# Keeping the residual in SBUF in front of a Fourier mixer, running the channel DFT group by group behind the fold, and placing two kinds of small work later in an RG-LRU output map

## The chip, the cores and the metric

The kernel runs on the 8 cores of one Trainium2 chip. Each core computes one of the 8 batch elements; the cores exchange nothing. The metric is the device time of the slowest core in microseconds (us). Every figure of the trace is from the slowest core of one profiled execution, core 4.

## The reference

A backbone of two layers works on 2048 latent tokens of 2048 channels per batch element (256 context tokens run beside them up to the first mixer). Each layer is: half-step SwiGLU, token mixer, half-step SwiGLU. The mixer of layer 0 is a bidirectional RG-LRU, that of layer 1 a grouped Fourier transform. Every sub-layer takes an RMSNorm of its input, shifts and scales it by adaLN terms, and adds the gated RMSNorm of its output to the residual stream x:

```python
def ffn_sublayer(x, g_pre, g_post, shift, scale, gate, w_in, w_out):
    y = swiglu(modulate(rmsnorm(x, g_pre), shift, scale), w_in, w_out)
    return x + MACARON * gate * rmsnorm(y, g_post)

def fourier_mixer(h, w_out):
    hg = h.reshape(bsz, n, N_FGROUPS, FGROUP).astype(jnp.float32)
    f = jnp.fft.fftn(hg, axes=(1, 3), norm='ortho').real
    return f.reshape(bsz, n, D_MODEL).astype(h.dtype) @ w_out
...
        hx = modulate(rmsnorm(x, g[2]), sh2, sc2)
...
        x = x + gt2 * rmsnorm(y, g[3])
```

So a sub-layer's residual update needs the norm of its whole output y, and the next pre-norm the norm of the whole updated x.

## The kernel before

Activations lie channel-major: 16 chunks of 128 channels (KC = 16, index m or kc) by tokens. The residual lives in DRAM (`xs`), sub-layer outputs too (`ys`). Tokens are worked in tiles of 1024 (two halves of 512). The program is written out by hand: the order in which Python emits instructions is the order on each engine, and waits are semaphores derived from tile accesses. DMAs issued by SP (SyncE) carry activations, those issued by POOL (GpSimd) weights and constants; each issuer's DMAs start in its program order, and an issuer that waits holds up all that stands behind it.

A normal feed-forward phase streams weights and lets the matmuls run; the residual update of the other tile is woven in step by step (`post_steps`: a piece of y and x of 128x512 is loaded to the ring `xl`, updated, stored, squared and summed).

Two places matter here.

**The RG-LRU output map** (`rglru`, function `mix_y`, called for tiles i = 0 and 1). For each of 16 output chunks m PE does 32 matmuls (`mix_mm`, L1013), ScalarE copies the result out of PSUM (L1119), SP stores it to `ys` (L1121), ScalarE squares it (L1126), and PE adds the squares up by a matmul with ones (L1132); that last matmul is kept in the list `pend` and comes one chunk later. While tile 0 is mapped, the residual of tile 0 is loaded to SBUF (`Resident.load_x`, L647, 16 tiles `xm`, two DMAs each); while tile 1 is mapped, `Resident.post` updates that residual, two chunks per m for m = 1 to 8: two VectorE operations (L668, L672), a square on ScalarE (L676), and the matmul with ones on PE (L682), which `post` issues at once. Then come the scale of the next norm, the modulated input of the feed-forward, and the stores of the residual.

**The front of the Fourier mixer.** The transform folds position t with 2048 - t. Tile 0 (positions 0 to 511 and 1536 to 2047) is folded inside the last feed-forward phase (`fold_steps(F, 0)`). After that phase `fourier` runs on an idle PE: `carry` (32 steps of `post_steps` for tile 1, positions 512 to 1535, with sums on PE, L414), the scale of the norm, `stage1` for the four position blocks of tile 0, the loads and folds of tile 1 (`fold_steps(F, 1)`, 16 steps), `stage1` for the blocks 4 to 8. `stage1(nb)` is the channel DFT: for one block of 128 positions all 8 channel groups, cosine part (L1348 with 128 columns, L1351 with one) to `U`, sine part (L1366) to `V`. Block 8 is the single position 1024. `stage2` is the position DFT of `U` with the constant `Cn` and of `V` with `Sn`; its first matmul of the sine part needs `V` and `Sn`. `Cn`, `Sn` and the first output weights `wf` are loaded by POOL ahead of `carry`.

Of the kernel before, what the change touches and what calls it, by code (L numbers as in the profile page):

```python
# [180 lines left out]
def build(nsub=6):  # L181
# [96 lines left out]
    hgb = S.sbuf("hgb", [128, 64], F32)  # L278
    qtb = S.sbuf("qtb", [128, 1], F32)
# [360 lines left out]
    class Resident:  # L640
# [21 lines left out]
        def post(self, m, slot):  # L662
# [21 lines left out]
            S.op("pe", stat, reads=[ry, r_const], writes=spair_res(slot))  # L684
# [35 lines left out]
    def rglru(W0, tl, hx, hcb, r_hxs, tiles):  # L720
# [384 lines left out]
        def mix_y(i, ky, sched):  # L1105
            pend = []
            for m in range(KC):
# [6 lines left out]
                while pend:  # L1114
                    pend.pop(0)()
# [41 lines left out]
        def begin():  # L1157
            for _ in range(yr.n - 1):
# [17 lines left out]
        sched = {m + 1: [lambda m=m, i=i: R.post(2 * m + i, kp[0]) for i in range(2)] for m in range(8)}  # L1176
# [3 lines left out]
        mix_y(1, ky, sched)  # L1180
# [64 lines left out]
    def fold_steps(F, t):  # L1245
        ta, tb, nb_ = ((0, 1536, 512), (512, 1024, 513))[t]
        q = []

        def load(kc):
            out = []  # L1250
            for (t0, w) in ((ta, 512), (tb, nb_)):
                b, rb, dn = xl.next()
                S.dma("sp", dn, lambda e, b=b, t0=t0, w=w: e.dma_start(out=b[:, :w], in_=xs[kc, :, t0:t0 + w]),
                      reads=X_s.r(kc, t0, w), writes=[rb])
                out += [b, rb, rb.gen]
            q.append(out)

        def mk(kc):
            def f():
# [3 lines left out]
                if kc + 2 < KC:  # L1263
# [3 lines left out]
                S.op("dve", lambda e: e.tensor_tensor(out=xa[:, :512], in0=xa[:, :512], in1=rsx[t][:, 0:512],  # L1267
                                                      op=ALU.mult), reads=[r_rsx[t]], writes=[ra])
                S.op("dve", lambda e: e.tensor_tensor(out=xb[:, :512], in0=xb[:, :512], in1=rsx[t][:, 512:1024],
                                                      op=ALU.mult), reads=[r_rsx[t]], writes=[rb])  # L1270
                if t == 0:
                    S.op("dve", lambda e: e.tensor_copy(out=xb[:, 512:513], in_=xa[:, 0:1]), reads=[ra], writes=[rb])
                else:
                    S.op("dve", lambda e: e.tensor_tensor(out=xb[:, 512:513], in0=xb[:, 512:513],
                                                          in1=rsx[0][:, 512:513], op=ALU.mult),
                         reads=[r_rsx[0]], writes=[rb])
                    S.op("act", lambda e: e.activation(out=F.hx[:, kc, 0:1], in_=xb[:, 0:1], func=AF.Identity,
                                                       bias=modcol(1, 3, kc, 0), scale=dercol(1, 1, 0, 0, kc)),
                         reads=[rb, r_der] + r_modq(1, 3), writes=[F.r_hx])
# [6 lines left out]
                S.op("act", lambda e: e.activation(out=F.H[t][0][:, kc, :], in_=pb[:], func=AF.Identity,  # L1286
                                                   bias=sh2[:, kc:kc + 1], scale=dercol(1, 1, 0, 0, kc)),
                     reads=[rp, r_der, r_sh2], writes=[F.r_H[t][0][kc]])
                S.op("act", lambda e: e.activation(out=F.H[t][1][:, kc, :], in_=xa[:, :512], func=AF.Copy,
                                                   scale=dercol(1, 1, 0, 0, kc)),  # L1290
                     reads=[ra, r_der], writes=[F.r_H[t][1][kc]])
# [355 lines left out]
```

How the kernel before makes its waits and increments, by code:

```python
    def _wait(self, stream, ev):  # L89
        if ev is None:
            return
        key, val = ev
        if self.seen[stream].get(key, 0) >= val or (stream == "pe" and key == "E_pe"):
            return
        self.seen[stream][key] = val
        self.eng[stream].wait_ge(self.sems[key], val)
# [16 lines left out]
    def op(self, stream, fn, reads=(), writes=()):  # L113
        self._deps(stream, reads, writes)
        ins = fn(self.eng[stream])
        key = "E_" + stream
        self.cnt[key] += 1
        ins.then_inc(self.sems[key], 1)
        ev = (key, self.cnt[key])
        self._commit(ev, reads, writes)
        return ev
# [1 line left out]
    def dma(self, stream, dsem, fn, reads=(), writes=()):  # L123
        self._deps(stream, reads, writes)
        key = "D_" + dsem
        sem = self._sem(key)
        inss = fn(self.eng[stream])
        if not isinstance(inss, (list, tuple)):
            inss = [inss]
        for ins in inss:
            ins.then_inc(sem, 16)
            self.cnt[key] += 16
        ev = (key, self.cnt[key])
        self._commit(ev, reads, writes)
        return ev
```

## Time and profile before

| | us |
|---|---|
| runs shown | 9951.44 (median), 9933.07, 11277.62 |
| profiled execution | 9958.34 |
| its span, slowest core (core 4) | 9957.0 |
| spans of the other cores | 9864.1 to 9951.5 |

The time of an execution is the span of the slowest core and 1.3 us around it. The run of 11277.62 is of a disturbed kind and is not compared with. PE (TensorE) is busy 89% of the span, so what can move is where it stands idle. The rows further down are read so: a timeline row has start, duration, engine, line of the kernel, operation and tiles, and in square brackets how long the engine stood idle before it and what ended that; rows named POOLq or SPq, or DMA_DIRECT2D on POOL, are issues of DMAs, not transfers. The granted clock PEclk is a share of 2.4 GHz; 0.5 is the lower level of 1.2 GHz.

### The profile page before, as it was taken

How to read it: one execution, taken by the hardware profiler on the slowest of the kernel's cores; microseconds unless marked ns; L12 is line 12 of the kernel's file. 1: busy time of each engine (PE TensorE's matmuls, PEld its weight loads, DVE VectorE, ACT ScalarE, POOL GpSimd, SP SyncE). 2: the span in 40 equal slices, each digit the busy share in tenths (PEclk: the TensorE clock that was granted, in tenths of full speed). 3: DMA queues.
4: the chain of work that ended last, by engine and by line, in shares of the span. 5: the costliest groups of instructions: out<-in, count | busy, mean ns of one | idle time of the engine just before them, and what ended most of it. 6: DMA issues, size and time to landing. Idle time of an engine off the chain costs nothing.

```text
span 9957.0 us, 124360 instructions; the slowest of 8 cores (9864.1 to 9957.0 us)
## 1 busy us (share of the span) xinstructions
PE 8893.2 (89%) x47440; PEld 4372.1 (44%) x48079; DVE 2410.6 (24%) x3408; ACT 2016.8 (20%) x2999; POOL 614.1 (6%) x983
## 2 busy tenths in 40 slices
PE   2999999997886889999999999999965499999994
PEld 1665555653332334444444444444423144444442
DVE  1111211213886212111211221122124322111102
ACT  1111111123775311111111111111113211110000
POOL 0000000000111000000000000000000000000000
PEclk9999999998998999999999999999977799999997
DMA  8778878887445677567766996677565676566545
GB/s 165 140 127 169 162 132 159 162 153 168 90 85 134 148 159 144 113 133 149 150 122 139 176 185 130 136 148 146 118 164 150 169 144 139 109 135 121 119 90 140
DMA packets 517609, 1399.41 MB, mean 141 GB/s; under 512 B 63640, under 2 KB 193816, under 8 KB 464032
## 3 DMA queue, kind: packets, MB, share of 16 engines
q0 software_dynamic: 152352, 830.83, 49.6%
q1 hardware_dynamic: 364672, 560.58, 19.1%
q8 instruction: 391, 6.41, 0.3%
q14 instruction: 194, 1.59, 0.1%
HBM read 1979.48 MB, written 221.25 MB: 221 GB/s over the span
## 4 chain that ended last, share of the span: by engine, by line
PE 79%; DMA 10%; ACT 3%; DVE 3%; issue 2%; SPq 1%; DVEq 0%; ACTq 0%; POOL 0%; POOLq 0%
PE PS L178 48%; PE PS L598 25%; PE PS L1013 2%; PE PS L798 1%; DMA w_36_90<-modw 1%; PE PS L883 1%; DVE gM_49_21458 L917 1%; DMA wfs<-ev_26_80 1%; PE PS L349 1%; SPq L647 1%; DMA wfs<-ev_27_81 0%; DMA ys<-ev_26_80 0%; DMA xl_21_75<-ys 0%; PE PS L393 0%; DVE gB_47_21456 L914 0%
## 5 line engine op out<-in xcount | busy, mean ns | idle before, releaser
L408 DVE TENSOR_TENSOR acc_16_70<-acc_16_70,sq_29_83 128x512 f32<-128x512 f32 (+1 forms) x135 | 87.4, 648 | 2007.7 <-ACT sq_29_83 L407 1957.1
L178 PE MATMUL PS<-hb_28306,w_90_28303 128*128 128x512 bf16 x2381 | 536.2, 384 | 4.8 <-ACT acc_16_70 L397 1.8
L178 PE MATMUL PS<-hb_28306,w_89_28302 128*128 128x512 bf16 x2315 | 521.6, 384 | 3.8 <-issue 0.5
L178 PE MATMUL PS<-hb_28306,w_88_28301 128*128 128x512 bf16 x2128 | 475.7, 382 | 15.1 <-DVE mods_3_45 L356 11.8
L178 PE MATMUL PS<-hb_28306,w_87_28300 128*128 128x512 bf16 x2127 | 476.9, 383 | 3.4 <-issue 0.5
L178 PE MATMUL PS<-hb_28306,w_91_28304 128*128 128x512 bf16 x2069 | 462.6, 382 | 2.5
L178 PE MATMUL PS<-hb_92,w_34_88 128*128 128x384 bf16 x2048 | 344.1, 330 | 45.4 <-ACT hb_92 L474 32.3
L178 PE MATMUL PS<-hb_92,w_36_90 128*128 128x384 bf16 x2176 | 361.3, 327 | 12.5 <-DVE mods_2_44 L356 12.3
L178 PEld LDWEIGHTS PS<-hb_28306,w_90_28303 128*128 128x128 bf16 x2432 | 239.4, 99 | 294.1 <-issue 33.0
L178 PE MATMUL PS<-hb_92,w_35_89 128*128 128x384 bf16 x2176 | 361.2, 327 | 1.5 <-ACT ev_28_82 L571 1.2
L178 PEld LDWEIGHTS PS<-hb_28306,w_89_28302 128*128 128x128 bf16 x2368 | 232.7, 99 | 283.7 <-issue 26.9
L178 PE MATMUL PS<-hb_92,w_33_87 128*128 128x384 bf16 x2048 | 341.0, 328 | 2.5 <-ACT ev_26_80 L571 2.5
L178 PEld LDWEIGHTS PS<-hb_28306,w_88_28301 128*128 128x128 bf16 x2176 | 213.0, 98 | 269.6 <-issue 25.2
L178 PEld LDWEIGHTS PS<-hb_28306,w_87_28300 128*128 128x128 bf16 x2176 | 213.4, 99 | 258.5 <-issue 16.8
L571 ACT ACTIVATE ev_28_82<-PS 128x512 f32<-128x512 f32 (+1 forms) x266 | 148.6, 559 | 840.2 <-PE PS L178 789.7
L571 ACT ACTIVATE ev_26_80<-PS 128x512 f32<-128x512 f32 (+1 forms) x262 | 145.9, 557 | 845.8 <-PE PS L178 797.4
L178 PEld LDWEIGHTS PS<-hb_28306,w_91_28304 128*128 128x128 bf16 x2112 | 206.9, 98 | 251.0 <-issue 15.4
L571 ACT ACTIVATE ev_27_81<-PS 128x512 f32<-128x512 f32 (+1 forms) x264 | 147.4, 558 | 827.4 <-PE PS L178 789.6
L178 PEld LDWEIGHTS PS<-hb_92,w_34_88 128*128 128x128 bf16 x2048 | 201.6, 99 | 181.3 <-issue 51.5
L178 PEld LDWEIGHTS PS<-hb_92,w_36_90 128*128 128x128 bf16 x2176 | 213.1, 98 | 154.2 <-issue 14.3
L178 PEld LDWEIGHTS PS<-hb_92,w_35_89 128*128 128x128 bf16 x2176 | 212.9, 98 | 144.0 <-issue 5.2
L598 PE MATMUL PS<-hid_28305,w_90_28303 128*128 128x512 bf16 x1164 | 263.9, 384 | 5.2 <-DVE hid_28305 L573 1.9
(763 smaller groups left out, 12355.1 us busy)
## 6 DMA issues: line engine op xcount, KB each, us to landing
w_90_28303<-win POOLq DMA_DIRECT2D x38, 1024.0 KB, 10.1
w_89_28302<-win POOLq DMA_DIRECT2D x37, 1024.0 KB, 9.9
w_35_89<-win POOLq DMA_DIRECT2D x34, 1024.0 KB, 10.9
w_36_90<-win POOLq DMA_DIRECT2D x34, 1024.0 KB, 10.7
w_87_28300<-win POOLq DMA_DIRECT2D x34, 1024.0 KB, 11.1
w_88_28301<-win POOLq DMA_DIRECT2D x34, 1024.0 KB, 11.0
w_91_28304<-win POOLq DMA_DIRECT2D x33, 1024.0 KB, 10.3
w_34_88<-win POOLq DMA_DIRECT2D x32, 1024.0 KB, 10.7
```

The source lines that it names most:

```text
L178: ins = e.matmul(out, l, r, start=(i == 0), stop=(i == n - 1))
L349: ins = e.matmul(o, w, scb[:, 2 * c:2 * c + 2], start=(c == 0), stop=(c == KC - 1))
L408: S.op("dve", lambda e: e.tensor_tensor(out=a, in0=a, in1=sb[:, :n], op=ALU.add), reads=[rsq], writes=[r_acc])
L571: S.op("act", lambda e, tb=tb, h=h, k=ks[0]: e.activation(out=tb[:, :n], in_=sbank(k, h, n), func=AF.Silu), reads=[rPS[2 * ks[0] + h]], wr ...
L598: ins = e.matmul(sbank(k, h, n), buf[:, (c - a) * 128:(c - a + 1) * 128], rhs(c, h), start=(c == 0), stop=(c == nk - 1))
L647: S.dma("sp", f"xr{m}", lambda e: [e.dma_start(out=self.xr[m][:, off:off + w], in_=src.ap[m, :, t0:t0 + w]) for (off, w, src, dst, t0, whi ...
L798: ins = e.matmul(sbank(k, b % 2, 512), buf[:, kk * 256 + o:kk * 256 + o + 128], hx[:, kk, b * 512:(b + 1) * 512], start=(kk == 0), stop=(k ...
L883: ins = e.matmul(PS[:, 3072 + h * 512:3584 + h * 512], wg(d, g), vcb[:, lo + h * 512:lo + (h + 1) * 512], start=True, stop=True)
L917: S.op("dve", lambda e: e.tensor_tensor_scan(out=f(gM[d]), data0=f(gA[d]), data1=f(gB[d]), initial=0.0, op0=ALU.mult, op1=ALU.add), reads= ...
L1013: ins = e.matmul(sbank(k, h, 512), buf[:, c * 128:(c + 1) * 128], zt[i][:, c, h * 512:(h + 1) * 512], start=(c == 0), stop=(c == KC - 1))
```

## The change

1. In `mix_y` of tile 0, `load_x(m)` no longer stands for all 16 chunks ahead of the loop: chunk m's load is issued in the loop behind the stores of chunk m.
2. `Resident.post` can hand its matmul with ones to the caller's list `pend`. In `mix_y` of tile 1 it does, so that these come behind the next chunk's 32 matmuls, beside the sum that was there already. `begin` loads 3 pieces of y ahead instead of 4, since a buffer is now held longer.
3. In `fourier`, the residual update of tile 1 is done by `Resident` on whole chunks of 1024 columns: 3 pieces of y and all 16 of x are queued on SP, x stays in SBUF (`xf`, in the room of `U`, `V`, `Cn` and `Sn`), and the stores of it follow. The fold of tile 1 reads `xf`; one of its two halves, the subtraction, goes to POOL. `c16` is the one column (position 1536) that the fold needs from tile 0, fetched for all chunks by one DMA.
4. `stage1` goes by channel group instead of position block. Groups 0 to 5 stand inside the fold, in pairs, behind its chunks 10, 12 and 14; groups 6 and 7 behind it. `Cn` and `Sn` are loaded behind the fold and behind the stores of the residual whose room they take.

```diff
-        for m in range(KC):
-            R.load_x(m)
-        mix_y(0, 3, {})
+        mix_y(0, 3, {m: [lambda m=m: R.load_x(m)] for m in range(KC)}, [])
...
-            S.op("pe", stat, reads=[ry, r_const], writes=spair_res(slot))
+            go = lambda: S.op("pe", stat, reads=[ry, r_const], writes=spair_res(slot))
+            if pend is None:
+                go()
+            else:
+                pend.append(go)
...
+        for m in range(KC):
+            if m < yr.n - 1:
+                R.load_y()
+            R.load_x(m)
...
+        ks = hold_slot()
+        rstd(accs[0], r_accs[0], 512, slot=ks)
+        for m in range(KC):
+            R.post(m, ks)
+        rstd(rsx[1], r_rsx[1], 512, ks)
+        held.discard(ks)
+        for m in range(KC):
+            R.store(m)
...
+        def fold1(m):
+            tb, rt, _ = yr.next()
+            S.op("dve", lambda e: e.tensor_tensor(out=tb[:, :1024], in0=xr[m][:], in1=rsx[1][:], op=ALU.mult),
+                 reads=[r_rsx[1], r_xr[m]], writes=[rt])
+            S.op("dve", lambda e: e.tensor_copy(out=tb[:, 1024:1025], in_=c16[:, m, :]), reads=[r_c16], writes=[rt])
...
+            S.op("dve", lambda e: e.tensor_tensor(out=pb[:], in0=tb[:, :512], in1=xv, op=ALU.add), reads=[rt], writes=[rp])
+            S.op("pool", lambda e: e.tensor_tensor(out=qb[:], in0=tb[:, :512], in1=xv, op=ALU.subtract), reads=[rt], writes=[rq])
...
+        for m in range(KC):
+            fold1(m)
+            if m == 9:
+                handover(r_xr[:9], r_Us + r_U8 + r_V)
+            if m >= 10 and m % 2 == 0:
+                for g in {10: (0, 1), 12: (2, 3), 14: (4, 5)}[m]:
+                    stage1(g)
+        handover(r_xr[8:13], [r_Cn])
+        handover(r_xr[13:] + yr.res[3:], [r_Sn])
         S.dma("pool", "fcn", lambda e: e.dma_start(out=Cn[:], in_=cn3), writes=[r_Cn])
...
+        stage1(6)
+        stage1(7)
-        for st in carry:
-            st()
```

Where the change moves instructions is seen best in the queues of the engines. In SP's queue at the start of the output map of tile 0, the kernel before has sixteen pairs of `xm` loads and then the stores of the loop; this is the end of the loads:

```order
L647 DMA xm_107_28320<-xs 128x512 x2
L647 DMA xm_108_28321<-xs 128x512 x2
L647 DMA xm_109_28322<-xs 128x512 x2
L1121 DMA ys<-ev_26_80 128x512
L1121 DMA ys<-ev_27_81 128x512
```

With the change the stores of a chunk stand ahead of one load (names count one lower, `xm_93` is the first residual chunk):

```order
L1045 DMA zt_80_22235<-zs 128x7x512 x4
L1124 DMA ys<-ev_25_79 128x512
L1124 DMA ys<-ev_26_80 128x512
L646 DMA xm_93_28306<-xs 128x512 x2
L1124 DMA ys<-ev_27_81 128x512
L1124 DMA ys<-ev_25_79 128x512
L646 DMA xm_94_28307<-xs 128x512 x2
```

On PE at the start of the output map of tile 1 (`zt` is the mixer's result, `wm` a weight; `sq` with `onesb` the sum over y, `ym` with `onesb` that over the residual), before:

```order
L1013 MATMUL PS<-zt_81_22236,wm_82_22237 128x512 x32
L1013 MATMUL PS<-zt_81_22236,wm_83_22238 128x512 x32
L1132 MATMUL PS<-sq_29_83,onesb_48 128x512 x2
L682 MATMUL PS<-ym_110_28323,onesb_48 128x512 x2
L682 MATMUL PS<-ym_111_28324,onesb_48 128x512 x2
L1013 MATMUL PS<-zt_81_22236,wm_84_22239 128x512 x32
```

and with the change, where the first two sums over the residual stand one chunk's 32 matmuls later:

```order
L1016 MATMUL PS<-zt_80_22235,wm_81_22236 128x512 x32
L1016 MATMUL PS<-zt_80_22235,wm_82_22237 128x512 x32
L1135 MATMUL PS<-sq_28_82,onesb_48 128x512 x2
L1016 MATMUL PS<-zt_80_22235,wm_83_22238 128x512 x32
L1135 MATMUL PS<-sq_29_83,onesb_48 128x512 x2
L681 MATMUL PS<-ym_109_28322,onesb_48 128x512 x2
L681 MATMUL PS<-ym_110_28323,onesb_48 128x512 x2
```

On POOL in front of the Fourier mixer, before, the constants follow the small fills at once:

```order
L1323 MEMSET hxx_59040 128x2048
L1324 MEMSET Ux_59051 128x1152
L1325 MEMSET Wx_59052 128x2048
L1326 DMA Wx_59052<-fwx 8x2048
L1327 DMA Cn_59043<-cn 128x9216
L1328 DMA cnx_59054<-cn 128x9
```

With the change sixteen subtractions of the fold (L1363, the last two shown) stand ahead of them:

```order
L1363 TENSOR_TENSOR sq_28_82<-yf_151_59076 128x512
L1363 TENSOR_TENSOR sq_29_83<-yf_152_59077 128x512
L1415 DMA Cn_59046<-cn 128x9216
L1416 DMA cnx_59057<-cn 128x9
L1417 DMA Sn_59053<-sn 128x8192
```

## Rows read from the trace of the kernel before

**Rows 1.** The page: its first line, and the chain that ended last by engine.

```profile
span 9957.0 us, 124360 instructions; the slowest of 8 cores (9864.1 to 9957.0 us)
...
PE 79%; DMA 10%; ACT 3%; DVE 3%; issue 2%; SPq 1%; DVEq 0%; ACTq 0%; POOL 0%; POOLq 0%
```

**Rows 2.** Windows: length, engines' busy time, granted clock, DMA share, GB/s.

```profile
2380.00:2440.00 60.00, 21.84 (x72) 6.28 (x70) 38.24 (x53) 20.23 (x26) 0.00 (x0) 0.60 0.92 292
3190.00:3226.00 36.00, 0.69 (x3) 0.28 (x3) 0.00 (x0) 2.33 (x4) 0.53 (x1) 0.55 0.95 275
3226.00:3330.00 104.00, 98.80 (x438) 44.17 (x446) 0.00 (x0) 30.92 (x44) 6.88 (x13) 0.96 0.65 137
3345.00:3452.00 107.00, 79.49 (x302) 31.75 (x306) 29.58 (x24) 31.22 (x40) 4.23 (x8) 0.89 0.52 143
3452.00:3546.00 94.00, 51.83 (x237) 22.37 (x241) 18.78 (x17) 35.56 (x41) 5.16 (x9) 0.77 0.92 196
7356.00:7488.00 132.00, 19.50 (x35) 3.90 (x35) 47.51 (x66) 25.55 (x39) 9.53 (x11) 0.53 0.82 244
7488.00:7500.00 12.00, 11.75 (x193) 11.47 (x193) 6.20 (x11) 8.80 (x10) 0.00 (x0) 0.73 0.62 176
7548.00:7562.00 14.00, 12.25 (x225) 12.28 (x227) 5.13 (x5) 5.68 (x6) 0.00 (x0) 0.84 0.00 1
```

**Rows 3.** Timeline, output map of tile 0: SP, ScalarE and PE around its third chunk.

```profile
3188.99 1.03 PE L1013 MATMUL PS<-zt_80_22235,wm_84_22239 128*128 128x512 bf16 x4
...
3215.17 0.42 SPq L1121 DMA_DIRECT2D ys<-ev_26_80  x1
...
3223.66 0.60 ACT L1119 ACTIVATE ev_26_80<-PS 128x512 f32<-128x512 f32 x1 [34.76 <-DMA ys<-ev_26_80]
...
3226.55 9.21 PE L1013 MATMUL PS<-zt_80_22235,wm_85_22240 128*128 128x512 bf16 x31 [0.22 <-issue]
```

**Rows 4.** Timeline of PE in the output maps of tile 0 and then tile 1.

```profile
3257.61 0.59 PE L1132 MATMUL PS<-sq_30_84,onesb_48 128*128 128x512 bf16 x2
...
3264.95 0.59 PE L1132 MATMUL PS<-sq_29_83,onesb_48 128*128 128x512 bf16 x2
...
3386.67 0.59 PE L1132 MATMUL PS<-sq_30_84,onesb_48 128*128 128x512 bf16 x2
...
3390.13 0.59 PE L682 MATMUL PS<-ym_111_28324,onesb_48 128*128 128x512 bf16 x2 [2.86 <-ACT ym_111_28324 L676]
...
3400.10 0.59 PE L1132 MATMUL PS<-sq_29_83,onesb_48 128*128 128x512 bf16 x2
```

**Rows 5.** Timeline of VectorE: residual updates of 1024 columns in the same map.

```profile
3337.12 1.22 DVE L668 TENSOR_TENSOR ym_112_28325<-ym_112_28325,acc_86_28299 128x1024 f32<-128x1024 f32 x1
...
3339.71 1.22 DVE L668 TENSOR_TENSOR ym_113_28326<-ym_113_28326,acc_86_28299 128x1024 f32<-128x1024 f32 x1
```

**Rows 6.** DMA issues from 3150 to 3560: KB each, median us from issue to landing.

```profile
ym_112_28325<-ys SPq DMA_DIRECT2D x3, 512.0 KB, 6.9
```

**Rows 7.** Timeline of PE, both ends of the Fourier mixer's front.

```profile
7346.36 9.66 PE L598 MATMUL PS<-hid_28305,w_91_28304 128*128 128x512 bf16 x44
...
7563.65 1.89 PE L178 MATMUL PS<-Sn_59050,V_59042 128*128 128x512 bf16 x8
```

**Rows 8.** Timeline of POOL and VectorE in the RG-LRU loop.

```profile
2611.87 4.50 POOL L922 TENSOR_TENSOR gM_50_21459<-gM_50_21459,gM_49_21458 128x2048 f32<-128x2048 f32 x1 [11.06 <-DVE gM_50_21459 L917]
...
2613.15 5.65 DVE L897 SCALAR_TENSOR_TENSOR gB_47_21456<-gB_47_21456,vcB_21463 128x2304 f32<-128x2304 f32 x1 [1.43 <-ACT gB_47_21456 L887]
...
2624.82 2.55 DVE L897 SCALAR_TENSOR_TENSOR gB_48_21457<-gB_48_21457,vcB_21463 128x2304 f32<-128x2304 f32 x1
```

**Rows 9.** DMA issues from 7340 to 7600, columns as in rows 6.

```profile
Cn_59043<-cn POOLq DMA_DIRECT2D x1, 2304.0 KB, 12.3
...
Sn_59050<-sn POOLq DMA_DIRECT2D x1, 2048.0 KB, 17.6
...
cnx_59054<-cn POOLq DMA_DIRECT2D x1, 2.2 KB, 12.0
```

More of the change, by code:

```diff
@@ L1113, in mix_y @@
                     mix_mm(m, i, k, range(KC))
-                while pend:
-                    pend.pop(0)()
+                for f in list(pend):
+                    f()
+                pend.clear()
                 load_wm(i * KC + m + 4)
@@ L1157, in begin @@
         def begin():
-            for _ in range(yr.n - 1):
+            for _ in range(yr.n - 2):
                 R.load_y()
@@ L1266, in f @@
                 assert ra.gen == ga and rb.gen == gb
[L1267 to L1279, printed above, removed]
+                S.op("dve", lambda e: e.tensor_tensor(out=xa[:, :512], in0=xa[:, :512], in1=rsx[0][:, 0:512],
+                                                      op=ALU.mult), reads=[r_rsx[0]], writes=[ra])
+                S.op("dve", lambda e: e.tensor_tensor(out=xb[:, :512], in0=xb[:, :512], in1=rsx[0][:, 512:1024],
+                                                      op=ALU.mult), reads=[r_rsx[0]], writes=[rb])
+                S.op("dve", lambda e: e.tensor_copy(out=xb[:, 512:513], in_=xa[:, 0:1]), reads=[ra], writes=[rb])
                 pb, rp, _ = ev.next()
@@ L1301, in fourier @@
         o += 4096
+        X0 = o
         U = sb_at("U", [128, 9, 1024], BF16, o)
@@ new lines, in stage1, with pe_u, pe_v @@
+        def stage1(g):
+            hs = [F.H[0][0], F.H[1][0]]
+            ms = [F.H[0][1], F.H[1][1]]
+            rp = [F.r_H[t][0][2 * g + jj] for t in range(2) for jj in range(2)]
+            rm = [F.r_H[t][1][2 * g + jj] for t in range(2) for jj in range(2)]
+            lhs = lambda H, nb, jj: H[nb // 4][:, 2 * g + jj, (nb % 4) * 128:(nb % 4) * 128 + 128]
+            ku = next_slot()
+            kv = next_slot()
+            def pe_u(e):
+                ins = None
+                for nb in range(9):
+                    w = lambda jj: lhs(hs, nb, jj) if nb < 8 else F.hx[:, 2 * g + jj, :]
+                    o = ku * 1024 + nb * 128 if nb < 8 else k8 * 1024
+                    for jj in range(2):
+                        e.matmul(PS[:, o:o + 128], w(jj), ccs[:, jj, 0:128], start=(jj == 0), stop=(jj == 1))
+                    o = kx * 1024 + nb * 8 + g
+                    for jj in range(2):
+                        ins = e.matmul(PS[:, o:o + 1], w(jj), ccs[:, jj, 128:129], start=(jj == 0), stop=(jj == 1))
+                return ins
+            S.op("pe", pe_u, reads=rp + [r_cc, F.r_hx], writes=spair_res(ku) + [rPS[2 * kx], rPS[2 * k8]])
+            gs = slice(g * 128, (g + 1) * 128)
+            S.op("act", lambda e: e.activation(out=U[:, 0:8, gs], in_=PS[:, ku * 1024:(ku + 1) * 1024].rearrange(
+                "p (b f) -> p b f", f=128), func=AF.Copy), reads=spair_res(ku), writes=[r_Us[g]])
+            S.op("act", lambda e: e.activation(out=U[:, 8, gs], in_=PS[:, k8 * 1024:k8 * 1024 + 128], func=AF.Copy),
+                 reads=[rPS[2 * k8]], writes=[r_U8[g]])
+            def pe_v(e):
+                ins = None
+                for nb in range(8):
+                    o = kv * 1024 + nb * 128
+                    for jj in range(2):
+                        ins = e.matmul(PS[:, o:o + 128], lhs(ms, nb, jj), ccs[:, jj, 129:257], start=(jj == 0), stop=(jj == 1))
+                return ins
+            S.op("pe", pe_v, reads=rm + [r_cc], writes=spair_res(kv))
+            S.op("dve", lambda e: e.tensor_copy(out=V[:, :, gs], in_=PS[:, kv * 1024:(kv + 1) * 1024].rearrange(
+                "p (b f) -> p b f", f=128)), reads=spair_res(kv), writes=[r_V[g]])
@@ L1376, in fourier @@
-        for nb in range(4):
-            stage1(nb)
-        for st in fold_steps(F, 1):
-            st()
-        for nb in range(4, 9):
-            stage1(nb)
+        stage1(6)
+        stage1(7)
+        handover(yr.res[:3], xl.res)
         S.op("dve", lambda e: e.tensor_copy(out=Ux[:, :, 0:8], in_=PS[:, kx * 1024:kx * 1024 + 72].rearrange(
```

125 lines of the change are left out of this document (55 added, 70 removed).

## The prediction, made before the change was run

> **What bounds the kernel now.** I read the page's chain of waits first: 79% of the 9957.0 us span runs through PE, 10% through DMA [rows 1]. So PE's matmuls set the time, the change leaves their number as it is, and it can only win where PE stands idle beside its three edits. The windows give the size of these places [rows 2]. From 3190 to 3226 PE is busy 0.69 of 36 us while the DMA engines are busy 0.95. From 3345 to 3452 it is busy 79.5 of 107 us. From 7356 to 7488 it is busy 19.5 of 132, and up to 7562 two blocks of 12 us and 14 us follow with 48 us between them. Then the timeline, for what ends each wait. In the output map of tile 0 PE stops at 3190.0 and goes on at 3226.55, because ScalarE waits 34.76 us for one store of y, which SP issues at 3215.17, behind 32 loads of the residual [rows 3]. In the map of tile 1 the period from one sum over y to the next is 3400.10 - 3386.67 = 13.43 us, where in that of tile 0 it is 3264.95 - 3257.61 = 7.34 us [rows 4]: behind the 32 matmuls PE waits 2.86 us for the square of the residual, and the rest of a period runs at less than the full clock, for the granted clock of this stretch is 0.89 [rows 2]. In front of the Fourier mixer the last feed-forward matmul ends at 7346.36 + 9.66 = 7356.02, and the first matmul that needs `V` and `Sn` starts at 7563.65 [rows 7]: 207.6 us, in which PE has 24.0 us of channel DFT (11.75 + 12.25 [rows 2]) and some sums.
>
> **Edit 1, the loads of the residual behind the stores.** The two stores of a chunk no longer queue behind 32 loads, so the fourth chunk can start when the third ends: 3226.55 - 3190.02 = 36.5 us at most. The price is that 8.4 MB now have to pass while PE works. In the idle stretch the DMA engines were busy 0.95 x 36 = 34 us; were all of that residual, the stretch from 3226 to 3330 would go from 0.65 x 104 = 68 to 102 us of 104 [rows 2]. It just fits, and the stores and weights are wanted a chunk or more later. SP now has one load of 0.5 MB ahead of each chunk's stores, a wait of about 2 us at 275 GB/s, with 7.3 us to hide in. Ends: 20 (the map becomes DMA-paced for part of its length) and 36.5. I take **34**, near the end that the store order gives, less something for the crowd.
>
> **Edit 2, sums one chunk later.** A chunk with the sums of two residual chunks is the 7.34 us period plus four matmuls of 512 columns; 32 + 2 of them make 7.34, so four cost 0.86, and the chunk is 8.2 us if nothing else binds. Eight chunks carry them: 8 x (13.43 - 8.2) = 41.8 us. What could bind next: VectorE needs 2 x 2.59 us a chunk [rows 5], below 8.2. DMA is busy 0.52 x 13.43 = 7.0 us a chunk, which is 0.85 of 8.2. The y pieces are fetched three ahead instead of four, and each load waits until the buffer's sum has run: from there 6.9 us of landing [rows 6], 2.6 of VectorE and about 3 of ScalarE make 12.5, against two chunks, 16.4. If the landing doubled, the chunk would be about 10 and the gain 27. Ends 20 and 42; I take **40**. The tail of this map (3452 to 3546, DMA busy 0.92 [rows 2]) stores the residual and loads the next weights. Its order stays, and it keeps its length.
>
> **Edit 3, the front of the Fourier mixer**, as a chain from 7356.0:
> - The scale and the first loads are as before. On SP 3 pieces of y and 16 of x now stand ahead of the fourth y: 19 x 0.524 = 10 MB. At 275 GB/s, as the residual loads of rows 2 went, that is 36 us; at 244 or 292 (the lowest and highest of the load stretches there) 41 or 34. Begun at about 7359, the fourth y lands at 7397.
> - Updates 3 to 15 go at VectorE's pitch of 2.59 [rows 5], 34 us, to 7431. The ring of 4 just covers a landing of 6.9 us. Square, sums and two steps of the scale: 5 us, 7436. The stores (8.4 MB, 31 us) run beside the fold and must be done for the first nine chunks before `U` is written; they are, near 7467.
> - The fold: VectorE has 1.22 for 1024 columns, about 0.7 for 512, and some 0.3 for the single column and gaps, 2.25 us. The subtraction on POOL is 4.50/4 = 1.13 us, by the row of 2048 columns [rows 8]. Whether the two run side by side decides. The rows say no: a VectorE operation with two SBUF operands that starts 1.3 us into POOL's takes 5.65 us, where the same form alone takes 2.55, that is, it ends as if begun when POOL's was over (2616.4) [rows 8]. So a chunk is 3.4 us if they never overlap, and 2.7 if only VectorE is held, since the subtraction and the addition become ready together and only the difference of 1.13 and 0.7 is added. I take 3.4, for 16 chunks 54 us; with 2.7 it is 43.
> - Three pairs of `stage1` inside the fold. They are not beside the fold: ScalarE's copies and VectorE's casts wait for PE, and the next chunk of the fold queues behind them. All 416 DFT matmuls took 24.0 us at clocks of 0.73 and 0.84 [rows 2]. A pair is a quarter: 6 us at that clock, 8.6 at the lower level, plus a cast of 1.2 and hand-overs. I take 9, 27 for three: 7436 + 54 + 27 = 7517.
> - Then `Cn`, its last column and `Sn` are issued, behind the sixteenth subtraction on POOL. `Sn` landed 17.6 us after its issue beside other traffic [rows 9]; 4.5 MB at 292 GB/s are 15. I take 17 and 1 for the issues: 7535. The last pair hides behind that.
>
> Gain 7563.65 - 7535 = **28 us**. Ends: none at all (244 GB/s, and pairs at 14 us, as they come with PE at the lower level and every copy in series), and 48 (292 GB/s, chunks of 2.25, pairs of 8).
>
> A rule bears on the fold. The Trainium skill, page "SBUF — State Buffer", section "Who interferes with whom", states that a VectorE instruction with two SBUF inputs and a GpSimd one that reads SBUF exclude each other for the whole instruction, and that the order of issue decides which is blocked. By it the chunk is 3.4 us, which the rows above show for one of the two orders; with the side-by-side reading (2.7) the sum below would be 11 us shorter.
>
> Costed at nothing: `c16`, 2048 elements fetched by SP at the start of the last feed-forward phase. A DMA of 1152 such elements landed after 12.0 us, and the large `Cn` ahead of it took as long [rows 9], so about 21 us at most; the fold of tile 0 behind it has a whole phase of 16 chunks to catch up. Without that cover VectorE would be late by these 21 us. The 8.4 MB that the old fold read again are gone with no gain of their own, since their time is in the chain.
>
> **Sum.** 9958.3 (the profiled execution) - 34 - 40 - 28 = 9856. The median of the runs shown lies 7 us lower, so 9849; I say **9850**. By the ends: 36.5 + 42 + 48 = 126 gives 9825, 20 + 20 + 0 gives 9911.
>
> **The rivals**, on the basis of the median.
> - *The front gains nothing.* Pairs and fold in series, then the constants, eat what the saved reads give: 9951 - 74 = 9877. For it: all three consumers wait in one queue order, and PE starts each pair after idling, at 0.55 of the clock (rows 2 show that value for idle stretches). Against: 8.4 MB less, and updates on 1024 columns at 2.59 us, where the 32 old steps took 132 us. Chance 0.17.
> - *POOL and VectorE overlap, or the constants come fast.* The front gains 45: 9951 - 119 = 9832. For: the two operands of the subtraction were read by nobody else in rows 8. Against: the held operation there. Chance 0.14.
> - *The sums still wait.* y lands too late with 3 ahead and a busier queue, edit 2 gives 10: 9879. Here the change does not do what it says. Against: 16.4 us for 12.5. Chance 0.07.
> - *DMA becomes the bound, and the kernel is slower.* If transfers in these places cannot exceed the 137 to 143 GB/s that the two maps show [rows 2], the 8.4 MB cost 61 us in the map of tile 0 against 36 saved; its neighbour, with the same 15 MB, gains nothing; and the front, whose 17 MB of loads are then read in 122 us and whose stores hold up `U` for another 61, ends near 7600 instead of 7563.65. 25 + 38 = 63 us more: 10014. It decides from the point where a chunk of the first map needs over 7.3 us of DMA. Against: 275 and 292 GB/s in the same rows. Chance 0.04.
>
> My forecast has the remaining 0.58. The range 9805 to 9900 takes in the forecast's ends but for the worst, the first three rivals, and the 18 us between the two undisturbed runs; the fourth rival and a part of the tails stay out. All ends together save 126 us, and 2% of 9951 is 199 us (about what a measurement of this kernel can tell from no change), so within 2% it is in nearly every case: faster by over 2% 0.02, within 0.96, slower 0.02.
>
> **What would show it.** Edit 1: ScalarE's copy in the map of tile 0 no longer waits some 35 us for a store, and the DMA share of the map nears 0.9. Edit 2: the residual's sums on PE have no wait on ScalarE, and the period is near 8.2. Edit 3: VectorE's update operations 2.6 us apart from the fourth on; in the fold, additions or subtractions longer than alone and a pitch of 3.4; three gaps of about 9 us on VectorE ended by PE; the first matmul on `Sn` released by its DMA. I would be wrong if the stores of y are late again behind single loads, if the subtraction runs beside the addition, or if `stage1` takes far more than 9 us a pair.

## The result, and the profile after

The changed kernel took 9818.26 and 9825.11 us, the kernel before 9933.07 and 9951.44 us: ratio 0.9879, 95% interval 0.9836 to 0.9921, some 120 us or 1.2% less. (The four runs of the change have a median of 10136.3 us, because in two of them one or both dies ran at a lowered clock, for which the forecast has no term; such dies are left out of every total below, and the profile shown is that of a later run of the same kernel without them.) The forecast was 9850 within 9805 to 9900, "within 2%" with 0.96. For these two times the direction and the range held; the gain was 120 us instead of 102, and its parts were not those of the forecast.

The page of the changed kernel, first line and chain:

```profile
span 9817.0 us, 124059 instructions; the slowest of 8 cores (9771.0 to 9817.0 us)
...
PE 77%; DMA 11%; DVE 4%; ACT 3%; issue 3%; SPq 1%; DVEq 0%; POOL 0%; ACTq 0%; POOLq 0%
```

PE's share of the chain fell from 79% to 77% [rows 1], though its matmuls are the same in number. The rows that follow are from core 3, whose front comes closest to the mean of the eight cores. PE in the output map of tile 0, third and fourth chunk, and then in tile 1 (start, us, engine, line, output<-inputs, count, idle before and its releaser):

```profile
3181.20 1.02 PE L1016 MATMUL PS<-zt,wm 128*128 128x512 bf16 x4
3188.48 1.01 PE L1135 MATMUL PS<-sq,onesb 128*128 128x512 bf16 x2 [6.25 <-ACT sq L1129]
...
3322.50 0.59 PE L1135 MATMUL PS<-sq,onesb 128*128 128x512 bf16 x2
3322.93 1.03 PE L681 MATMUL PS<-ym,onesb 128*128 128x512 bf16 x4
3323.80 7.07 PE L1016 MATMUL PS<-zt,wm 128*128 128x512 bf16 x32
3330.70 0.59 PE L1135 MATMUL PS<-sq,onesb 128*128 128x512 bf16 x2
```

The stop of 36.5 us [rows 3] has become one of 6.25 us. In tile 1 the period is 3330.70 - 3322.50 = 8.20 us where it was 13.43 [rows 4], and no sum of the residual (L681) waits for ScalarE. The waits are only a part of the 5.23 us: before, PE stood idle 2.86 and 0.35 us in a period, and the 32 matmuls behind that took 8.76 us, which now take 7.07:

```profile
3391.08 0.59 PE L682 MATMUL PS<-ym_112_28325,onesb_48 128*128 128x512 bf16 x2 [0.35 <-ACT ym_112_28325 L676]
3391.51 8.76 PE L1013 MATMUL PS<-zt_81_22236,wm_83_22238 128*128 128x512 bf16 x31
```

So 3.2 us of a period were the waits, and most of the other 2 went with the granted clock, which was 0.89 over this stretch [rows 2] and is 1.00 in the windows below, where PE no longer stands idle. (31 of the 32 matmuls were recorded in the row of before.)

The wait that was left of the first comes from ScalarE's own queue:

```profile
3186.83 0.60 ACT L1122 ACTIVATE ev<-PS 128x512 f32<-128x512 f32 x1 [5.71 <-DMA ys<-ev]
...
3190.03 0.60 ACT L1122 ACTIVATE ev<-PS 128x512 f32<-128x512 f32 x1 [1.69 <-DMA ys<-ev]
...
3193.58 0.60 ACT L1122 ACTIVATE ev<-PS 128x512 f32<-128x512 f32 x1 [2.95 <-DMA ys<-ev]
```

Three copies still wait 10.4 us in all for a store of y, where one waited 34.76. The stores themselves are slow to land while the first loads and the weights pass; the DMA issues of core 3 from 3178 to 3196 show (KB each, median us from issue to landing):

```profile
ys<-ev SPq DMA_DIRECT2D x6, 256.0 KB, 6.9
```

The windows of the two maps (columns as in rows 2) show DMA at 0.88 and 0.86 of its time (0.65 and 0.52 before), and that PE still stands idle at the end of the second map, which the change does not touch:

```profile
3200.00:3307.00 107.00, 102.23 (x467) 45.72 (x466) 7.01 (x6) 30.49 (x43) 6.88 (x13) 0.98 0.88 217
3307.00:3390.00 83.00, 80.94 (x376) 36.58 (x375) 41.69 (x35) 41.90 (x52) 5.29 (x10) 1.00 0.86 214
3390.00:3470.00 80.00, 49.68 (x249) 22.42 (x248) 10.59 (x11) 29.30 (x33) 4.63 (x8) 0.81 1.02 235
```

The front of the Fourier mixer, both ends on PE; the last y matmul ends at 7224.80 + 7.29 = 7232.09, and the front is 7398.92 - 7232.09 = 166.8 us (207.6 before [rows 7]):

```profile
7224.80 7.29 PE L597 MATMUL PS<-hid,w 128*128 128x512 bf16 x33
...
7398.92 1.89 PE L178 MATMUL PS<-Sn,V 128*128 128x512 bf16 x8 [1.12 <-DMA Sn<-sn]
```

VectorE between them:

```profile
7271.00 1.23 DVE L667 TENSOR_TENSOR yf<-yf,acc 128x1024 f32<-128x1024 f32 x1 [21.06 <-DMA yf<-ys]
...
7304.10 1.28 DVE L671 SCALAR_TENSOR_TENSOR xf<-yf,der,xf 128x1024 f32<-128x1024 f32 x1 [0.17 <-DVE yf L667]
7310.22 1.23 DVE L1356 TENSOR_TENSOR yf<-xf,rsx 128x1024 f32<-128x1024 f32 x1 [4.84 <-ACT rsx L398]
...
7311.88 0.69 DVE L1362 TENSOR_TENSOR ev<-yf 128x512 f32<-128x512 f32 x1 [0.17 <-DVE yf L1358]
7312.48 2.29 DVE L1356 TENSOR_TENSOR yf<-xf,rsx 128x1024 f32<-128x1024 f32 x1
...
7315.82 2.30 DVE L1356 TENSOR_TENSOR yf<-xf,rsx 128x1024 f32<-128x1024 f32 x1
...
7345.21 0.69 DVE L1362 TENSOR_TENSOR ev<-yf 128x512 f32<-128x512 f32 x1 [0.17 <-DVE yf L1358]
7350.64 1.23 DVE L1404 CAST V<-PS 128x1024 bf16<-128x1024 f32 x1 [4.74 <-PE PS L1401]
...
7354.32 1.22 DVE L1356 TENSOR_TENSOR yf<-xf,rsx 128x1024 f32<-128x1024 f32 x1
...
7382.86 0.69 DVE L1362 TENSOR_TENSOR ev<-yf 128x512 f32<-128x512 f32 x1 [0.17 <-DVE yf L1358]
```

The fourth update starts 38.9 us after the last y matmul, the last ends at +73.3, the fold begins at +78.1 and VectorE is through with it at 7383.55, +151.5. A chunk of the fold has a pitch of 3.33 us (7312.48 to 7315.82), and its multiplication over 1024 columns takes 2.29 us except where POOL was done before: 1.23 in the first chunk, 1.22 behind a pair of `stage1`. A pair holds VectorE from 7345.90 to 7354.32, 8.4 us; the two others take 7.6 each. POOL in the same stretch:

```profile
7311.91 1.78 POOL L1363 TENSOR_TENSOR sq<-yf 128x512 f32<-128x512 f32 x1 [74.02 <-DVE yf L1358]
...
7318.64 1.73 POOL L1363 TENSOR_TENSOR sq<-yf 128x512 f32<-128x512 f32 x1 [1.61 <-DVE yf L1358]
...
7385.72 0.54 POOL L1417 DMA_DIRECT2D Sn<-sn  x1
```

Over the eight cores of each profile the parts have these means. Tile 0 of the map is counted from the first sum over y to the first of tile 1, tile 1 from there to the sum of its 11th chunk, the end from there to its last sum:

```
us                      before   after   gain   forecast
tile 0 of the map        156.3   127.5   28.8     34
tile 1, ten chunks       124.4    82.7   41.7     40
the end of tile 1         66.1    64.9    1.2      0
front of the mixer       209.7   166.3   43.4     28
sum                                     115.1    102
```

The whole kernel, by the mean span of a core in the set of runs of this profile, went from 9915.2 to 9798.1, 117 +- 15 us less: within that interval the four parts are all of it.

### The profile page after: what moved, and what is told of

It is laid out like the page before. It is cut to its first block, busy times and chain, and to the rows that moved or that the text cites. A ratio compares the mean times of both kernels' runs of the same rounds, so it can differ in the third digit from the quotient of the medians.

```text
span 10446.2 us, 124059 instructions; the slowest of 8 cores (10271.6 to 10446.2 us)
## 1 busy us (share of the span) xinstructions
PE 9459.1 (91%) x47440; PEld 4509.1 (43%) x48079; DVE 2401.4 (23%) x3349; ACT 2013.8 (19%) x2986; POOL 642.3 (6%) x999
## 4 chain that ended last, share of the span: by engine, by line
PE 80%; DMA 10%; ACT 3%; DVE 3%; issue 3%; SPq 1%; DVEq 0%; POOL 0%; ACTq 0%; POOLq 0%
PE PS L178 49%; PE PS L597 26%; DMA xl<-xT 2%; DMA wfs<-ev 2%; PE PS L1016 2%; DMA w<-modw 1%; PE PS L801 1%; DMA outT<-xl 1%; DMA xl<-xs 1%; DMA xl<-fwf 1%; PE PS L886 1%; DVE gM L920 1%; DMA ys<-ev 1%; PE PS L348 1%; DMA wa<-modw 1%
## 5 line engine op out<-in xcount | busy, mean ns | idle before, releaser
L178 PE MATMUL PS<-hb,w 128*128 128x512 bf16 (+1 forms) x24983 | 5427.1, 382 | 133.4 <-DVE mods L355 52.1
L178 PEld LDWEIGHTS PS<-hb,w 128*128 128x128 bf16 x25344 | 2572.6, 102 | 2954.7 <-issue 1441.2
L597 PE MATMUL PS<-hid,w 128*128 128x512 bf16 (+1 forms) x12503 | 2702.3, 381 | 40.3 <-DMA w<-wout 10.7
L597 PEld LDWEIGHTS PS<-hid,w 128*128 128x128 bf16 x12672 | 1286.6, 102 | 1455.9 <-issue 690.8
L572 DVE TENSOR_TENSOR hid<-ev,PS 128x512 bf16<-128x512 f32 (+1 forms) x792 | 509.2, 643 | 3888.0 <-PE PS L178 3801.2
L570 ACT ACTIVATE ev<-PS 128x512 f32<-128x512 f32 (+1 forms) x792 | 402.8, 558 | 2772.7 <-PE PS L178 2613.9
L603 ACT ACTIVATE ev<-PS 128x512 f32<-128x512 f32 (+1 forms) x288 | 162.8, 565 | 1930.7 <-PE PS L597 1930.7
L801 PE MATMUL PS<-hx,wi 128*128 128x512 bf16 x1985 | 480.5, 388 | 26.2 <-ACT hcb L700 22.4
L554 POOL DMA_DIRECT2D w<-win x396 | 211.1, 533 | 4117.7 <-PE PS L178 3691.6
L506 DVE SCALAR_TENSOR_TENSOR xl<-xl,der,xl 128x512 f32<-128x512 f32 (+2 forms) x352 | 239.0, 679 | 133.2 <-DMA xl<-xT 52.7
L1016 PE MATMUL PS<-zt,wm 128*128 128x512 bf16 x1002 | 231.9, 388 | 9.2 <-DVE zt L1025 2.9
## 6 DMA issues: line engine op xcount, KB each, us to landing
w<-modw POOLq DMA_DIRECT2D x112, 1024.0 KB, 10.4
```

Source lines behind the costliest of these rows:

```text
L178: ins = e.matmul(out, l, r, start=(i == 0), stop=(i == n - 1))
L506: S.op("dve", lambda e, off=off, w=w, which=which: e.scalar_tensor_tensor(out=xb[:, off:off + w], in0=yb[:, off:off + w], scalar=dercol(l, ...
L554: S.dma("pool", dn, lambda e, buf=buf, j=j: e.dma_start(out=buf[:], in_=win[l, f, j]), writes=[rb])
L570: S.op("act", lambda e, tb=tb, h=h, k=ks[0]: e.activation(out=tb[:, :n], in_=sbank(k, h, n), func=AF.Silu), reads=[rPS[2 * ks[0] + h]], wr ...
L572: S.op("dve", lambda e, tb=tb, h=h, k=ks[1], j=j: e.tensor_tensor(out=W.hid[:, j, h * n:(h + 1) * n], in0=tb[:, :n], in1=sbank(k, h, n), o ...
L597: ins = e.matmul(sbank(k, h, n), buf[:, (c - a) * 128:(c - a + 1) * 128], rhs(c, h), start=(c == 0), stop=(c == nk - 1))
```

## The experiments

In what follows a kernel's total is the mean span of a core, less that of the kernel before in the same set of runs, with a 95% interval; a part is the mean over the cores of its profile.

**The changed kernel again**, in two sets.

> The changed kernel once more. Theory: its undisturbed time is 1.2% below the kernel before, about 120 us (ratio 0.988), of which 29 us come from the first tile of the RG-LRU map, 43 us from its second tile and 43 us from the front of the Fourier mixer. Rival: the gain of the first profile's undisturbed part is given back later in the layer, and the ratio is above 0.992 (less than 80 us).

> The changed kernel a third time, as the measure for the two beside it. Theory: 1.2% below the kernel before (118 to 124 us), its front 163 to 167 us. Rival: under 1%.

Measured: -122.7 +- 7.3 and -117.2 +- 15.0 us, 1.2% both times; the front 166.3 us.

**Each edit alone.** The first:

```diff
-        for m in range(KC):
-            R.load_x(m)
-        mix_y(0, 3, {})
+        mix_y(0, 3, {m: [lambda m=m: R.load_x(m)] for m in range(KC)})
```

> The kernel before with the first of the three edits alone: the residual's loads issued group by group behind the map's stores. Theory: the store's wait for the 4th y chunk's ring buffer is what they caused, so the first tile of the map takes 138 us instead of 166 and the kernel is 29 us faster (ratio 0.997). Rival: the loads arrive later, so that the second tile's first update waits for them, and less than 10 us is left.

The second is `post` with its list `pend`, and `begin` with `yr.n - 2` loads, in the kernel before:

> The kernel before with the second edit alone: the norm sums of the residual put on TensorE one matmul group later, with one y load fewer ahead. Theory: a pair of groups then takes 8.2 us in place of 13.4 for 8 chunks, the second tile 83 us in place of 126, and the kernel is 43 us faster (ratio 0.9957). Rival: with the first tile's loads still ahead of the stores, y chunks land late and the wait moves to the y loads; then less than 20 us.

The third is the changed kernel with these two undone:

> The changed kernel with both map edits undone, so that only the front of the Fourier mixer is changed. Theory: the front takes 164 us where it took 207.6, so the kernel is 43 us faster (ratio 0.9957). By the sum worked out beforehand it would be 28 us (0.9972), by the rival in which the front gains nothing 0 us. If the three single edits add up, this and the two others give 115 to 120 us together.

Measured: tile 0 takes 127.8 us with the loads alone (the mean of cores 0, 1, 6 and 7, whose granted clock there was 0.93 to 0.96; the other four had 0.78 to 0.79; the expectation's 138 and 166 us count some 10 us more on either side), ten chunks of tile 1 83.7 with the sums alone, the front 166.7 with the front alone, and with the sums alone and the front alone the other parts stay within 2 us of before. So each edit does its own part and none needs another. The totals were -37.0 +- 7.4, -50.3 +- 11.1 and -49.8 +- 9.2, some 7 to 10 us above each part and 137 together against 123 for all three in the same set; the intervals allow for that, and which of it is more than scatter stays open. The sums alone, at the place of rows 4:

```profile
3361.37 0.59 PE L1136 MATMUL PS<-sq,onesb 128*128 128x512 bf16 x2
3361.81 1.03 PE L682 MATMUL PS<-ym,onesb 128*128 128x512 bf16 x4
...
3369.58 0.59 PE L1136 MATMUL PS<-sq,onesb 128*128 128x512 bf16 x2
```

8.21 us, without a wait, though the loads still stand ahead of the stores in tile 0.

**Do POOL and VectorE exclude each other in the fold?** The subtraction goes to VectorE:

```diff
-            S.op("pool", lambda e: e.tensor_tensor(out=qb[:], in0=tb[:, :512], in1=xv, op=ALU.subtract), ...
+            S.op("dve", lambda e: e.tensor_tensor(out=qb[:], in0=tb[:, :512], in1=xv, op=ALU.subtract), ...
```

> The changed kernel with the subtraction of the fold of tile 1 on VectorE in place of POOL. Theory (a VectorE operation with two SBUF operands and a POOL one on SBUF exclude each other, so POOL's time is added to VectorE's): a chunk of the fold takes 2.85 us (1.22 + 0.3 + 2 x 0.66) where it took 3.33, and the front is 16 x 0.48 = 8 us shorter (167 to 159 us). Rival (POOL takes work off VectorE): a chunk gets 0.66 us longer less what POOL's turn costs now, and the front is the same or up to 8 us longer.

A chunk on VectorE:

```profile
7347.43 1.22 DVE L1356 TENSOR_TENSOR yf<-xf,rsx 128x1024 f32<-128x1024 f32 x1
...
7349.01 0.69 DVE L1362 TENSOR_TENSOR ev<-yf 128x512 f32<-128x512 f32 x1
7349.62 0.69 DVE L1363 TENSOR_TENSOR sq<-yf 128x512 f32<-128x512 f32 x1
7350.22 1.22 DVE L1356 TENSOR_TENSOR yf<-xf,rsx 128x1024 f32<-128x1024 f32 x1
```

With one more operation on VectorE its chunk is shorter, 2.79 us in place of 3.33, and every multiplication takes 1.22. So POOL's time was added to VectorE's, as the theory says, and the rival falls. The front is 153.9 us, 12 less than 166.3. The fold has 5.4 of that and not 16 x 0.54 = 9, since four of its 16 multiplications were not held in the changed kernel either, and those chunks get longer by the subtraction. The larger rest shows on POOL's queue, which no longer has subtractions ahead of the constants:

```profile
7379.35 0.54 POOL L1415 DMA_DIRECT2D Cn<-cn  x1 [113.80 <-DVE yf L1358]
...
7404.19 0.53 POOL L1417 DMA_DIRECT2D Sn<-sn  x1 [23.76 <-ACT hb L1289]
```

POOL had issued `Cn` 25 us before, as soon as the fold was through with its room, and `Sn` landed alone, 8.1 us after its issue for 13.7 (means); the experiment after the next has that by itself. The total (-123.5 +- 16.9) is too coarse to show 12 us.

**Are the pairs of `stage1` beside the fold or in series with it?**

```diff
-            if m >= 10 and m % 2 == 0:
-                for g in {10: (0, 1), 12: (2, 3), 14: (4, 5)}[m]:
-                    stage1(g)
...
-        stage1(6)
-        stage1(7)
+        for g in range(8):
+            stage1(g)
```

> The changed kernel with all eight groups of the channel DFT behind the fold, none inside it. Theory (the pairs are in series with the fold and hold up Cn and Sn): the fold ends 25 us sooner (3 pairs of 8 us), Sn lands 8 us before the last group is done, and the front is bound by eight groups of 4 us behind the fold: 8 to 10 us shorter than 167 us. Rival (the pairs are hidden beside the fold): the fold ends when it did and six more groups stand behind it, 24 us of which some 9 hide behind Sn: the front is 15 us longer.

The front is 156.3 us, 10 less (total -124.0 +- 15.5). PE behind the fold:

```profile
7407.00 0.27 PE L1384 MATMUL PS<-ccs,ha 128*128 128x128 bf16 x2 [0.51 <-ACT U L1393]
7410.04 0.27 PE L1384 MATMUL PS<-ccs,ha 128*128 128x128 bf16 x2 [0.51 <-ACT U L1393]
...
7423.63 2.10 PE L178 MATMUL PS<-Cn,U 128*128 128x512 bf16 x9 [1.62 <-DVE Ux L1418]
```

In series, as the theory says: without the six groups the fold takes 21 us less (52.3 for 73.6), where hidden pairs would have left it as it was, and the stage behind it only 13 more. A group takes 3.04 us here in place of the 4 expected. The windows show the granted clock: 0.78 within a pair inside the fold of the changed kernel (core 3), where PE stands idle between the pairs, and with all eight groups in one go 0.77 in the first 8 us and 1.00 in the next 8 (core 0):

```profile
7360.00:7367.50 7.50, 6.33 (x104) 6.03 (x102) 2.29 (x2) 3.92 (x6) 1.12 (x1) 0.78 0.00 0
```

```profile
7396.00:7404.00 8.00, 6.54 (x105) 6.22 (x106) 1.96 (x3) 4.22 (x7) 6.20 (x8) 0.77 0.63 228
7404.00:7412.00 8.00, 6.97 (x149) 6.68 (x150) 3.57 (x3) 2.64 (x5) 0.00 (x0) 1.00 0.99 412
```

The first matmul of the second stage is released by VectorE here and no longer by a transfer.

**The constants.**

```diff
-        handover(r_xr[8:13], [r_Cn])
+            if m == 12:
+                handover(r_xr[8:13], [r_Cn])
+                S.dma("pool", "fcn", lambda e: e.dma_start(out=Cn[:], in_=cn3), writes=[r_Cn])
...
-        S.dma("pool", "fcn", lambda e: e.dma_start(out=Cn[:], in_=cn3), writes=[r_Cn])
```

> The changed kernel with the load of Cn issued behind the 13th chunk of the fold, where its room is free, and not behind the 16th. Theory (Cn and Sn share the transfer rate, 4.5 MB in 13 us): Sn alone lands 9 us after its issue and the front is 4 us shorter than 167 us. Rival: Sn's landing has a delay of its own, 13 us whatever stands ahead, and the front stays.

The front is 162.6 us, 4 less, although its loads took 1.8 longer; counted from the end of the fold it is 5.8 less. The total (-121.6 +- 20.9) is too coarse to show either. The DMA issue of `Sn`, KB and us from issue to landing, in the change (core 3) and then in this kernel (core 4):

```profile
Sn<-sn POOLq DMA_DIRECT2D x1, 2048.0 KB, 13.1
```

```profile
Sn<-sn POOLq DMA_DIRECT2D x1, 2048.0 KB, 8.0
```

The 13 us are no delay of its own: without `Cn` just ahead of it `Sn` lands after 8.0 us.

**All of it together**: subtraction on VectorE, `Cn` early, `hx` as 16 resources instead of one (so that a group depends on its own two chunks alone), a group behind each chunk, and its copies out of PSUM one chunk later:

```diff
-        F.r_hx, r_Cn, ... = after([Res(x) for x in "hx Cn Sn Ux Wx cc Cx".split()], p0)
+        F.r_hx = after([Res(f"hx{m}") for m in range(KC)], p0)
...
         for m in range(KC):
             fold1(m)
...
+            if m >= 9:
+                if evac:
+                    evac()
+                evac = stage1(m - 9)
```

> The changed kernel with subtraction on VectorE, Cn issued behind the 13th chunk, the column hx in 16 pieces, one group of the channel DFT behind each chunk of the fold from the 10th on, and its copies out of PSUM one chunk later, so that VectorE does not stand behind PE. Theory: the three pairs of 8 us are gone but for their casts (1.2 us each), a chunk is 2.85 us, Sn lands 9 us after its issue: the front is 135 to 140 us in place of 167 and the kernel 27 to 32 us faster than the changed one. Rival (PE at its lower level needs over 4 us a group, and paces the fold): 150 us.

> The version with the rearranged front (subtraction on VectorE, Cn earlier, one group of the channel DFT behind each chunk from the 10th on) once more, on one chip with the changed kernel. Theory: its front took 144 us where that of the changed kernel took 165, and nothing gives that back, so it is 20 us faster than the changed kernel and 140 us (1.4%) faster than the kernel before. Rival: the clock or a later wait takes some back, less than 10 us against the changed kernel.

The front took 144 us in the first profile and 141.6 in the second, 25 less than the change, 2 to 4 over the expected upper end. The total is -141.3 +- 13.9 in the first set and in the second -142.4, where the change beside it had -117.2. That is 25 us, as the part says; the interval of this difference is as wide as the difference itself (+- 28), so the part carries it. What is left of the rival can be seen on VectorE:

```profile
7342.38 1.22 DVE L1406 CAST V<-PS 128x1024 bf16<-128x1024 f32 x1
...
7348.97 1.23 DVE L1406 CAST V<-PS 128x1024 bf16<-128x1024 f32 x1 [2.59 <-PE PS L1397]
...
7359.49 1.23 DVE L1406 CAST V<-PS 128x1024 bf16<-128x1024 f32 x1 [2.59 <-PE PS L1397]
```

Inside the fold every second cast still waits 2.6 us for PE.

**The front by stages.** These are the stages of the front in the experiments on it, means over the eight cores of each profile (in the last row of its second run): from the end of the last y matmul to the fold, the fold until VectorE is through with it, and from there to the first matmul on `Sn`. The first stage has the same instructions in all of them, so its differences are scatter of the loads.

```
us                              to the fold   fold   to Sn   front
the change                          76.6      73.6    16.0   166.3
subtraction on VectorE              76.2      68.2     9.4   153.9
all groups behind the fold          74.9      52.3    29.1   156.3
Cn early                            78.4      74.0    10.2   162.6
all of it together                  74.0      55.7    12.0   141.6
```

**The neighbouring place.** In the end of tile 1, too, a store of y stands behind the residual's. The same order there, on top of the last version:

```diff
             R.pre(m, 0, 0, 2, pdst2)
-            R.store(m)
+            if m < 6:
+                R.store(m)
...
         mix_y(1, ky, sched, pend)
+        for m in range(6, KC):
+            R.store(m)
```

> The same version, and in the map of tile 1 the stores of the residual's chunks 7 to 16 behind the last store of y (edit 1's order, in the neighbouring place: there PE stands idle 36 us for a store of y that SP issues behind six of the residual's). Theory: PE ends that map 36 us sooner; the hidden layer of the next phase has to wait for the 10 late stores, 5.2 MB or 18 us at 290 GB/s, of which the first group of matmuls hides about 12; so 25 to 30 us faster than the version without it. Rival: the DMA engines are busy 1.02 of that stretch, so the bytes set its length whatever their order, and the wait only moves to the first weights or the first hidden chunk: 0 to 5 us.

The end of the map shrank from 65.7 to 37.7 us, 28 less, and the kernel by 5 (-147.2 +- 17.2 against -142.4, which does not tell 5 us from none). PE at the end of the map in the version without this edit, then with it, and the operation that it waited for (core 5 of both):

```profile
3461.34 1.01 PE L1135 MATMUL PS<-sq,onesb 128*128 128x512 bf16 x2 [34.32 <-ACT sq L1129]
```

```profile
3433.15 1.01 PE L1135 MATMUL PS<-sq,onesb 128*128 128x512 bf16 x2 [5.78 <-ACT sq L1129]
3436.41 36.77 PE L178 MATMUL PS<-hb,w 128*128 128x512 bf16 x160 [1.42 <-ACT acc L396]
3494.89 8.92 PE L178 MATMUL PS<-hb,w 128*128 128x512 bf16 x32 [21.71 <-DVE hid L572]
```

```profile
3493.27 1.48 DVE L572 TENSOR_TENSOR hid<-ev,PS 128x512 bf16<-128x512 f32 x2 [58.01 <-DMA xs<-xm]
```

The rival was right: a 34 us wait has become one of 5.8 and one of 21.7, since the hidden layer lies where the residual was and the late stores have to be through first. The DMA engines were busy 1.02 of this stretch in the changed kernel, and here they are busy 0.98 of it up to the end of the second wait:

```profile
3433.00:3495.00 62.00, 38.72 (x195) 17.45 (x196) 1.79 (x4) 6.69 (x8) 1.61 (x3) 0.80 0.98 206
```

There the bytes set most of the length, and their order mainly the place of the wait; some 7 us of the 28 were left.

## Why the prediction was right, and where it was not

The step that failed is the sum of edit 3: it gives the front 28 us, and the front gained 43.4. Its chain of waits was the right one; its largest term, the fold with its pairs, was set at 54 + 27 = 81 us and took 73.6, the stretch ahead of the fold at 80 and took 76.6, and the stretch behind it at 18 and took 16.0. Edit 1 was off by 5 us the other way; that the sum of the parts, 115 us for 102, is not further off is partly luck.

**Edit 1: right in kind, 34 became 29.** The copies wait for the stores of single chunks while the first loads crowd in (5.71, 1.69 and 2.95 us). I had allowed 2.5 us for the crowd, and it took 8: the sum counts the 2 us that a load holds up a store in SP's queue, and not that the store then lands only after 6.9. The forecast that the bytes just fit was right: DMA share 0.88 for "nears 0.9".

**Edit 2: right**, 41.7 for 40, with a period of 8.20 for 8.2; three pieces of y ahead are enough even where the loads of tile 0 are left as they were. The rival "the sums still wait" falls.

**Edit 3: the chain was right link by link, its end 12 us too late.** From the end of the last y matmul:

```
us after the last y matmul    forecast   core 3
4th update of the residual       41       38.9
last update ends                 75       73.3
fold begins                      80       78.1
VectorE through with the fold   161      151.5
first matmul on Sn              179      166.8
```

The most mis-sized term is that of fold and pairs, 54 + 27 = 81 forecast and 73.4 measured on this core. I counted POOL's time into all 16 chunks, but where a chunk begins a run (the first, and the one behind each pair) POOL is idle and the multiplication takes 1.22 and not 2.29, which makes 4 us; and a pair costs 7.6 to 8.4, not 9, which makes 3. Next to it `Sn`, which landed 13.1 us after its issue; 17 had been taken over from rows 9, a landing in other traffic. The rate was taken low, too, 275 GB/s for 320 in the stretch of the loads:

```profile
7232.00:7270.00 38.00, 5.57 (x11) 1.09 (x10) 8.73 (x8) 8.69 (x10) 5.13 (x4) 0.57 0.95 320
```

Two more microseconds come from the row of before: its core had the shortest front of its profile, 207.6 for a mean of 209.7. Two of the workings do not follow from their own figures. The DFT matmuls of rows 2 make 11.75 x 0.73 + 12.25 x 0.84 = 18.9 us at full clock, so a pair, a quarter of them, would take 9.4 us at the lower level and not 8.6; measured was a clock of 0.78, so this did not matter. And the ends of edit 3, none and 48, come to some 7 and 53 us by its own terms.

**The rivals.** The measured time, 9818 to 9825, lies nearest to "POOL and VectorE overlap, or the constants come fast" (9832), and the front's gain, 43.4, nearest to its 45, but its first half did not happen: the exclusion holds in every chunk that follows another, and taking the subtraction off POOL ended it. The exclusion that the Trainium skill, page "SBUF — State Buffer", section "Who interferes with whom", states is thus what this trace shows (2.29 us for 1.22 on VectorE, 1.73 on POOL). The second half did in part: `Sn` came 4 us sooner after its issue, of the 15 that the sum was short. "DMA becomes the bound" falls for these three places, whose stretches moved 214 to 320 GB/s; in the end of tile 1 transfers do set the length, as the last experiment showed. "The front gains nothing" falls, but what spoke for it was so: pairs, fold and constants do stand in series, and 25 us more were to be had there.

## What to carry to other kernels

Where two engines take turns on a piece, cost the piece as the sum of the two, and look for the pieces at which one of them is idle; an operation moved to the second engine can make the chain longer than it was on the first. Before work that stands in series is put between pieces of a loop, ask which engine's queue it joins: here PE did not need VectorE, but the cast behind it held up the next piece. Before transfers are reordered, read the DMA share of the stretch: at 0.65 the reordering of edit 1 gained 29 us of 36, at 1.02 the same order mainly moved the wait.

## What the runs showed of the hardware

- VectorE with two SBUF operands and POOL on SBUF took turns to the end of the operation: 1.22 + 1.07 us of waiting for a multiplication of 1024 columns, and 1.73 us for a POOL subtraction of 512 columns that became ready together with an addition of 0.69.
- The loads of this front ran at 320 GB/s over 38 us, above the 244 to 292 of the stretches in rows 2.
- A DMA issue on POOL's queue is as late as the computing ahead of it: without the subtractions `Cn` went out 119.7 us after the last y matmul instead of 151.3 (means), with no other edit.
- The granted clock of the same matmuls depended on how they were strung: 0.78 in a pair of groups with idle time before it (7.6 to 8.4 us a pair), 1.00 in the later part of a go of all eight groups (3.04 us a group); and in the output map 0.89 with a wait in each period and 1.00 without (8.76 and 7.07 us for 32 matmuls).
- A 256 KB store took 6.9 us to land while loads and weights kept the DMA engines busy (share 0.87 from 3178 to 3200); 2 MB landed after 8.0 us, and after 13.1 behind 2.3 MB issued just before.
